# Head norms inside their own projections, and four joints between stages of a transformer pair on one Trainium2 core

## The chip, the cores and the metric

The kernel runs on 1 core of one Trainium2 chip. The metric is device time in microseconds from start to end of one execution on that core; the median over runs is given. Lower is better.

## The reference, cut to what matters

Two transformer blocks follow each other on 512 tokens of width 1024, all in fp32. The first block is a hybrid mixer (state space branch, dilated attention, pooling) with a feed-forward part; the second has four layers (window attention, latent attention, matrix LSTM, window attention) over 512 latent and 256 context tokens. The change touches four places of it:

```python
# first block, dilated attention: 12 heads of 128, each query and key head normed
qh = _rms(q.reshape(b, S, 12, 128), q_norm_w)
kh = _rms(k.reshape(b, S, 12, 128), k_norm_w)
# for each of 3 dilations: o, lse = attention(qh, kh, vh); then a softmax over the lse
# second block, every layer
h_l = rmsnorm(x_lat, g_pre) * (1.0 + sc_l) + sh_l
h_c = rmsnorm(x_ctx, g_pre) * (1.0 + sc_c) + sh_c      # over 256 context tokens
y_l, y_c = mixer(h_l, h_c)
x_lat = x_lat + gt_l * rmsnorm(y_l, g_post)
# layer 1, latent attention: two small norms ahead of two projections
q  = rmsnorm(q_a, g_qa) @ w_uq          # rank 256
kv = rmsnorm(kv_a, g_kva) @ w_ukv       # rank 128
o  = softmax(q k^T) v;   y = (o * silu(z)) @ w_out
# layer 3: y = (window_attention(rope(q), rope(k), v) * silu(z)) @ w_out, latent tokens only
```

## The kernel before, in words

All five engines run hand-written streams; they meet only through semaphores. Every fp32 product is made of three matmuls (`products`, L478 to L480): high part by high, high by low, low by high. ScalarE makes the high part of a weight slot of 2048 columns (`refill_hi`, L473), GpSimd the low part (L465), and SyncE's queue loads raw slots in a ring of three, each when TensorE is done with the slot before it in its place.

`dense` (from L508) is the projection routine. It walks over tiles; a tile is up to 512 columns by 8 chunks by 3 matmuls in one PSUM bank of a ring of `n_banks`. ScalarE copies each tile out (`act_tile`), which frees its bank (`tile_free`); refills of the coming slots stand at fixed tiles on ScalarE's queue. Guests (`Side`) put steps of their own behind tile t on each engine: `on_tensor`, `on_scalar`, `on_vector`, `within` (between the chunks of a tile), `early_scalar` (before the tile's copy), `after_vector`. `lead=2` computes the first two tiles together, chunk by chunk, and `rhs_ready` names a semaphore that a chunk of a tile has to wait for. `ada` puts the products of the modulation (L940 on VectorE, L871 for its transfers on ScalarE's queue) beside the tiles: ScalarE issues the next transfer, and copies the next tile, only when VectorE has used a place of the ring.

*First block, dilated attention* (`dilated_attention`, from L2000). Four projections j = 0 to 3 of 11 tiles each: tiles 0 to 5 are three query and three key heads, 6 to 9 values, 10 the rows of the third value head (`v_rows`), which TensorE has to transpose. Projections 0 and 1 host 8 and 4 slots of modulation. `HeadNorms` (from L1487) norms the six heads: squares on ScalarE (L1504), sums over partitions by a matmul with `ones` on TensorE (L1525), logarithm (L1510), exponential (L1515), the product on VectorE (L1543); it also transposes the V rows (L1530) and places them (L1538). The norms of projection j are the guest of projection j + 1, so those of 3 have no host: behind projection 3 the engines meet (`end_stage`, L383 to L402), walk through the eleven steps with filler matmuls around them (`keep_busy`, L381), and meet again. Then `group_attention` (from L1553) runs 16 units: scores (L1573), mask and minimum (L1617), exponential (L1639), scaling (L1630), transposes (L1581), copy (L1646), values (L1591).

*Into layer 0* (`LayerInBeside`, from L2708), guest of the last feed-forward projection: ScalarE squares the eight context chunks, VectorE adds them in SBUF (`tally_context`, L2753) behind tile 3, and TensorE sums the total over partitions in tile 4 behind chunk 2 (L2565). ScalarE then makes the root (L2571, L2572), and VectorE and ScalarE norm the context before VectorE takes tile 4 (L2367). VectorE also tallies the latent squares (L2745).

*Layer 1's joints.* `LatentSteps` (from L3276) makes the two small norms beside the projection of `z`: sums on TensorE (L3306) in banks 6 and 7, root 0 at its step 3, root 1 at step 5 (L1034, L1037; L3296 signals). `pair_attention` (from L1656) has 24 pairs of units; of the six pairs of two heads the fourth (last latent block) and the sixth (last context block) end with `finish` on VectorE (L3141, L753, L754: gate and split). Behind it TensorE runs 11 fillers (L1729) and all engines meet. Then `layer_cross` (from L3075) loads the residual (L3093), runs the projection `Bo` and crosses into the next layer.

*Layer 3's start of attention.* `AttentionStart` (from L1806) is the guest of the projection of `z` in 8 tiles: the scores of pairs 0 and 1 (L1879) behind tiles 4 and 5, VectorE's masks and minima (L1897) at tiles 5 and 6, four exponentials (L1913) behind the copy of tile 6, the first scaling (L1906) at tile 7. Window attention proper starts when tile 7 has been copied.

Of the kernel before, what the change touches and what calls it, by code (L numbers as in the profile page):

```python
# [23 lines left out]
P = 128  # L24
# [1462 lines left out]
class HeadNorms(Side):  # L1487
# [3 lines left out]
    STEPS = 11  # L1491

    def __init__(self, k, block, qkv, v, v_rows, squares, rstd, weights):
        self.k, self.qkv, self.v, self.v_rows = k, qkv, v, v_rows
        self.squares, self.rstd, self.weights = squares, rstd, weights
        self.squared, self.summed, self.logs, self.rooted, self.turned, self.normed = (
            k.sem_named(f"norm_{x}") for x in ("squared", "summed", "logs", "rooted", "turned", "normed"))

    def on_scalar(self, act, t):
        k = self.k  # L1500
        if t < 6:
            if t >= 2:
                act.wait_ge(self.summed.sem, self.summed.at(t - 1))
            act.activation(self.squares[:, t % 2], self.qkv[:, t, :], ACT.Square).then_inc(self.squared.sem, 1)  # L1504
        if t == 2 and self.normed.base:

            act.wait_ge(self.normed.sem, self.normed.at(0))
# [9 lines left out]
    def on_tensor(self, pe, t):  # L1517
        k = self.k
        if t == 1 and self.normed.base:
            pe.wait_ge(self.normed.sem, self.normed.at(0))  # L1520
        if 1 <= t < 7:
            pe.wait_ge(self.squared.sem, self.squared.at(t))
            if t >= 3:
# [3 lines left out]
        if t == 8:  # L1527
            pe.wait_ge(self.logs.sem, self.logs.at(5))
            for b in range(4):
                last = pe.transpose(k.psum[:, 6, b * P:(b + 1) * P], self.v_rows[:, b * P:(b + 1) * P],  # L1530
                                    k.cst("ident"))
            last.then_inc(self.turned.sem, 1)

    def on_vector(self, dve, t):
        k = self.k
        if t == 9:
            dve.wait_ge(self.turned.sem, self.turned.at(1))
            dve.tensor_copy(self.v[:, :, 256:384], k.psum[:, 6, :].rearrange("p (b n) -> p b n", b=4)) \  # L1538
                .then_inc(self.normed.sem, 1)
        if t == 10:  # L1540
# [5 lines left out]
    def over(self):  # L1546
        for x in (self.squared, self.summed, self.logs, self.rooted):
            x.stage_over(6)
        self.turned.stage_over(1)
        self.normed.stage_over(7)  # L1550


def group_attention(k, block, units, temp):  # L1553
# [6 lines left out]
    n, wide = len(units), 1280  # L1560
    row = k.at("group_row", temp, [P, 2, wide])
# [2621 lines left out]
```

## Time and profile before

| | |
|---|---|
| median of 3 runs | 2894.9 us (2893.01 to 2900.22) |
| the profiled execution's own time | 2897.45 us |
| its span, first to last instruction | 2895.7 us |
| granted TensorE clock, mean | 0.984 |
| TensorE busy | 2744.1 us, 95% |
| VectorE, ScalarE, GpSimd busy | 1555.8, 1231.5, 989.9 us |
| DMA | 293.73 MB, mean 101 GB/s |

Times in the views are microseconds from the first instruction. PE is TensorE, DVE VectorE, ACT ScalarE, POOL GpSimd. A name such as L1525 is the line of the kernel before. A TensorE row gives start and duration as modelled; matmuls overlap, so the distance of two starts tells what one costs. fp32 operands that are not split show as two records for each matmul. `[2.63 <-ACTq L3296]` at the end of a row: the engine stood idle for 2.63 us before it, until that was done.

### The profile page before, as it was taken

The numbers are of one execution on the slowest core, as the hardware profiler recorded it, in microseconds if no ns is written. First come the engines' busy times: TensorE is split into PE (matmuls) and PEld (weight loads), VectorE is DVE, ScalarE is ACT, GpSimd is POOL, SyncE is SP. The second block draws the span as 40 slices with busy tenths as digits, with TensorE's granted clock in tenths as the row PEclk, the third lists the DMA queues.
The fourth block names the chain that finished last, engine by engine and source line by source line (L and its number), as shares of the span: only waits on it lengthen the run. The fifth ranks groups of instructions, "written<-read, shape, count | busy, mean of one in ns | idle before, by whom it ended". The sixth has DMA issues, their size and how long they took to land.

```text
span 2895.7 us, 39337 instructions
## 1 busy us (share of the span) xinstructions
PE 2744.1 (95%) x15712; PEld 2268.5 (78%) x15712; DVE 1555.8 (54%) x3047; ACT 1231.5 (43%) x2139; POOL 989.9 (34%) x729
## 2 busy tenths in 40 slices
PE   6988989989999999999999999999999999999997
PEld 4766878868878888878977778677898878788785
DVE  6678292053653978772358451245446237752684
ACT  4335224554223322233268464544343236553682
POOL 3611565402545444433323333200234330143322
PEclk8999999999999999999999999999999999999998
DMA  8312462211232556633200121100221231124102
GB/s 320 134 42 85 174 258 88 88 44 44 102 131 102 218 204 233 218 117 113 98 30 2 59 88 73 58 1 1 92 98 59 95 124 48 70 88 138 45 2 73
DMA packets 54294, 293.73 MB, mean 101 GB/s; under 512 B 4512, under 2 KB 8928, under 8 KB 24288
## 3 DMA queue, kind: packets, MB, share of 16 engines
q1 hardware_dynamic: 22464, 163.59, 15.7%
q10 hardware_dynamic: 31648, 127.63, 11.7%
q8 instruction: 125, 2.05, 0.3%
q14 instruction: 57, 0.47, 0.0%
HBM read 268.10 MB, written 17.86 MB: 99 GB/s over the span
## 4 chain that ended last, share of the span: by engine, by line
PE 60%; DVE 6%; ACT 3%; issue 2%; POOL 1%; DMA 0%; PEldq 0%; PEld 0%; DVEq 0%; ACTq 0%; POOLq 0%
PE psum L478 15%; PE psum L480 15%; PE psum L479 15%; PE psum L1879 3%; PE psum L1926 2%; PE psum L1937 2%; PE psum L3924 2%; PE psum L1688 2%; PE psum L1711 2%; PE psum L1692 1%; PE psum L1700 1%; POOL w_lo L465 1%; DVE pair_row L1897 1%; DVE pair_prob L1906 1%; ACT pair_prob L1913 1%
## 5 line engine op out<-in xcount | busy, mean ns | idle before, releaser
L465 POOL TENSOR_TENSOR w_lo<-raw,w_hi 128x512 fp32r<-128x512 f32 x612 | 852.9, 1426 | 1569.0 <-ACT w_hi L473 1569.0
L478 PE MATMUL psum<-a_hi,w_hi 128*128 128x512 f32 (+2 forms) x1880 | 702.5, 374 | 32.6 <-DVE a_lo L1091 16.7
L479 PE MATMUL psum<-a_lo,w_hi 128*128 128x512 f32 (+2 forms) x1880 | 689.4, 367 | 0.0
L480 PE MATMUL psum<-a_hi,w_lo 128*128 128x512 f32 (+2 forms) x1880 | 689.3, 367 | 0.0
L478 PEld LDWEIGHTS psum<-a_hi,w_hi 128*128 128x128 f32 (+1 forms) x1880 | 355.2, 189 | 106.0 <-issue 17.9
L479 PEld LDWEIGHTS psum<-a_lo,w_hi 128*128 128x128 f32 (+1 forms) x1880 | 355.4, 189 | 61.6 <-issue 3.8
L480 PEld LDWEIGHTS psum<-a_hi,w_lo 128*128 128x128 f32 (+1 forms) x1880 | 355.0, 189 | 59.5
L473 ACT ACTIVATE w_hi<-raw 128x2048 fp32r<-128x2048 f32 x153 | 292.4, 1911 | 171.6 <-DMA raw<-stream 131.5
L478 PE MATMUL psum<-w_hi,a_hi 128*128 128x256 f32 (+1 forms) x608 | 196.6, 323 | 2.4 <-POOL w_lo L465 2.2
L940 DVE SCALAR_TENSOR_TENSOR ada_temp<-ada_ring,psum 128x1024 f32<-128x1024 f32 x160 | 185.7, 1217 | 18.0 <-ACT psum L1063 14.7
L479 PE MATMUL psum<-w_lo,a_hi 128*128 128x256 f32 (+1 forms) x608 | 192.4, 316 | 0.0
L480 PE MATMUL psum<-w_hi,a_lo 128*128 128x256 f32 (+1 forms) x608 | 192.4, 316 | 0.0
L1897 DVE CUSTOM_DVE_ANT_0 pair_row<-psum,pair_mask,neg_sinks 128x512 f32<-128x512 f32 (+1 forms) x160 | 115.8, 748 | 80.1 <-PE psum L1879 72.3
L940 DVE SCALAR_TENSOR_TENSOR ada_temp<-ada_ring,ada_rows 128x1024 f32<-128x1024 f32 x80 | 133.0, 1722 | 34.2 <-DVEq L1440 16.0
L1913 ACT ACTIVATE pair_prob<-pair_row,pair_stat 128x513 f32<-128x513 f32 (+1 forms) x160 | 114.7, 718 | 26.8 <-PE psum L1926 19.1
L478 PEld LDWEIGHTS psum<-w_hi,a_hi 128*128 128x128 f32 x608 | 115.8, 190 | 12.6 <-POOL w_lo L465 2.9
L479 PEld LDWEIGHTS psum<-w_lo,a_hi 128*128 128x128 f32 x608 | 115.8, 190 | 8.7 <-issue 1.4
L480 PEld LDWEIGHTS psum<-w_hi,a_lo 128*128 128x128 f32 x608 | 115.8, 190 | 7.6
L1879 PE MATMUL psum<-gk,gq 64*128 64x128 f32 (+1 forms) x960 | 95.3, 331 | 7.4 <-ACT gz L3174 3.9
L478 PE MATMUL psum<-hid_hi,w_hi 128*128 128x512 f32 x256 | 100.6, 393 | 0.0
L479 PE MATMUL psum<-hid_lo,w_hi 128*128 128x512 f32 x256 | 99.9, 390 | 0.0
L480 PE MATMUL psum<-hid_hi,w_lo 128*128 128x512 f32 x256 | 99.8, 390 | 0.0
(475 smaller groups left out, 4770.9 us busy)
## 6 DMA issues: line engine op xcount, KB each, us to landing
raw<-stream SPq DMA_DIRECT2D x153, 1024.0 KB, 4.8
ada_ring<-ada ACTq DMA_DIRECT2D x72, 1024.0 KB, 6.4
x_in<-xres ACTq DMA_DIRECT2D x3, 3072.0 KB, 10.3
xres<-x_in ACTq DMA_DIRECT2D x3, 2048.0 KB, 6.9
partner<-gq ACTq DMA_DIRECT2D x4, 1024.0 KB, 9.9
xres<-x_in ACTq DMA_DIRECT2D x1, 3072.0 KB, 9.3
own_raw<-stream SPq DMA_DIRECT2D x3, 1024.0 KB, 4.9
xres<-x_in ACTq DMA_DIRECT2D x3, 1024.0 KB, 4.9
```

Of the source, the lines that this page charges most:

```text
L465: last = pool.tensor_tensor(k.lo_of(s)[:, cols], k.raw_of(s)[:, cols], k.hi_of(s)[:, cols].bitcast(F32), ALU.subtract)
L473: act.activation(k.hi_of(s), k.raw_of(s), ACT.Copy).then_inc(k.hi_ready, 1)
L478: pe.matmul(out, lhs[0], rhs[0], start=start, stop=False)
L479: pe.matmul(out, lhs[0], rhs[1], start=False, stop=False)
L480: return pe.matmul(out, lhs[1], rhs[0], start=False, stop=stop)
L940: dve.scalar_tensor_tensor(self.temp[:, self.products % 2], self.ring[:, place, c], 1.0, self.used_rows[:, w], ALU.mult, ALU.mult, accum_o ...
L1688: pe.matmul(score(u)[:, col:col + cols], q, keys, start=True, stop=False)
L1711: last = pe.matmul(value_bank(u), units[u]["pv"][j], prob_t[:, u % n_t, j * P:(j + 1) * P], start=j == 0, stop=j == n_blocks - 1)
L1879: last = pe.matmul(score(u)[:, col:col + cols], q, keys, start=True, stop=True)
L1897: dve.tensor_tensor_reduce(row[:, u % 4, 1:1 + w], score(u), mask[:, un["mask"]:un["mask"] + w], 1.0, un["sink"], ALU.add, ALU.min, stat[: ...
L1913: act.activation(prob[:, u % 4, 0:1 + width(u)], row[:, u % 4, 0:1 + width(u)], ACT.Exp, bias=stat[:, 0, u % 4:u % 4 + 1], scale=-1.0, acc ...
L1926: last = pe.transpose(turn_place(u)[:, j * P:(j + 1) * P], prob[:, u % 4, 1 + j * P:1 + (j + 1) * P], k.cst("ident"))
```

## The change

It has six parts in the code.

1. `HeadNorms(j)` is now the guest of projection j itself. Its squares wait for the copy of their tile. The transposes of V rows leave it: they are made behind tile 0 of projection j + 1 (`turn_rows`, bank 7) and placed at tile 1 (`place_rows`); those of projection 3 inside `group_attention`, behind its first scores and ahead of the second unit on VectorE. The stage of its own, its two meetings and its 17 fillers are gone; the load of the attention's tables is issued between projections 2 and 3; the first scores wait for the norms of projection 3.
2. `tally_context` keeps its running sum in PSUM; the matmul over the total stands behind chunk 6 of tile 4, not 2.
3. `pair_attention` ends without fillers and meeting. The chunks of `Bo` wait for the `finish` that makes them, the residual's load for the last one, the weights' own slot for the last values; `Bo` computes its first two tiles together.
4. `LatentSteps` sums the second norm in banks 4 and 5 at step 3, and ScalarE makes both roots at step 4 (two logarithms each, one wait, the exponentials).
5. In layer 3 `AttentionStart` stands one tile later, and its first scaling comes behind the last tile.
6. `layer_cross` takes `lead` from its caller: 1 for layer 0 as before, 2 for `Bo`, 2 for `Co` as before.

The diff, cut to its core:

```diff
 class HeadNorms(Side):
@@ on_scalar
         if t < 6:
+            act.wait_ge(k.tile_free.sem, self.tile_free + t + 1)
             if t >= 2:
                 act.wait_ge(self.summed.sem, self.summed.at(t - 1))
             act.activation(self.squares[:, t % 2], self.qkv[:, t, :], ACT.Square).then_inc(self.squared.sem, 1)
@@ on_tensor
-        if t == 1 and self.normed.base:
-            pe.wait_ge(self.normed.sem, self.normed.at(0))
+        if t == 0 and self.rows_of is not None:
+            turn_rows(k, pe, self.rows_of, self.tile_free)
         if 1 <= t < 7:
             pe.wait_ge(self.squared.sem, self.squared.at(t))
+            if t == 2 and self.rows_of is not None:
+                pe.wait_ge(k.sem_named("rows_placed").sem, k.sem_named("rows_placed").at(1))
...
-        if t == 8:
-            pe.wait_ge(self.logs.sem, self.logs.at(5))
-            for b in range(4):
-                last = pe.transpose(k.psum[:, 6, b * P:(b + 1) * P], self.v_rows[:, b * P:(b + 1) * P],
-                                    k.cst("ident"))
-            last.then_inc(self.turned.sem, 1)
@@ on_vector
+        if t == 1 and self.rows_of is not None:
+            place_rows(k, dve, self.v_before)
         if t == 9:
-            dve.wait_ge(self.turned.sem, self.turned.at(1))
-            dve.tensor_copy(self.v[:, :, 256:384], k.psum[:, 6, :].rearrange("p (b n) -> p b n", b=4)) \
-                .then_inc(self.normed.sem, 1)
-        if t == 10:
             for r in range(6):
                 dve.wait_ge(self.rooted.sem, self.rooted.at(r + 1))
...
+def turn_rows(k, pe, rows, rows_in):
+    pe.wait_ge(k.tile_free.sem, rows_in)
+    for b in range(4):
+        last = pe.transpose(k.psum[:, 7, b * P:(b + 1) * P], rows[:, b * P:(b + 1) * P], k.cst("ident"))
+    last.then_inc(k.sem_named("rows_turned").sem, 1)
+
+def place_rows(k, dve, v):
+    turned = k.sem_named("rows_turned")
+    dve.wait_ge(turned.sem, turned.at(1))
+    dve.tensor_copy(v[:, :, 256:384], k.psum[:, 7, :].rearrange("p (b n) -> p b n", b=4)) \
+        .then_inc(k.sem_named("rows_placed").sem, 1)
@@ group_attention, scores(u)
             if u:
                 pe.wait_ge(masked.sem, masked.at(u))
+            else:
+                pe.wait_ge(*heads_normed)
+                pe.wait_ge(k.tile_free.sem, k.tile_free.at(-1))
...
         scores(0)
+        last_rows(pe)
...
+                if u == 1:
+                    last_placed(dve)
@@ pair_attention, end of TensorE's stream and of the stage
-        pe.wait_ge(masked.sem, masked.at(2 * n))
-        k.keep_busy(pe, k.psum[:, 0, :], 11)
...
-                pairs[p - 4]["finish"](dve)
+                pairs[p - 4]["finish"](dve).then_inc(finished.sem, 1)
...
-    k.end_stage(block)
+    return ends
@@ AttentionStart
+    def after_vector(self, dve):
+        if self.at + 3 >= self.n_tiles:
+            self.scale_probs(dve, 0)
@@ dilated_attention
-        dense(k, block, [f"qkv{j}"], tiles, act_tile=take, ada=ada.of((8, 4)[j]) if j < 2 else None, barrier=j == 3,
+        dense(k, block, [f"qkv{j}"], tiles, act_tile=take, ada=ada.of((8, 4)[j]) if j < 2 else None, barrier=False,
               n_banks=6, side=side)
...
-        k.keep_busy(pe, k.psum[:, 0, :], 6)
-        for t in range(side.STEPS):
-            side.on_tensor(pe, t)
-        k.keep_busy(pe, k.psum[:, 0, :], 11)
...
-    k.end_stage(block)
@@ LayerInBeside
-            so_far = self.squares_c[:, 0] if c == 1 else self.total_c[:]
-            dve.tensor_tensor(self.total_c[:], so_far, self.squares_c[:, c], ALU.add).then_inc(self.tallied_c.sem, 1)
+            so_far = self.squares_c[:, 0] if c == 1 else self.context.rstd
+            dve.tensor_tensor(self.total_c[:] if c == KC - 1 else self.context.rstd, self.squares_c[:, c], so_far,
+                              ALU.add).then_inc(self.tallied_c.sem, 1)
...
-        if (t, j) == (4, 2):
+        if (t, j) == (4, 6):
@@ gqa_layer, host
-              n_banks=n_banks, barrier=False, side=start(8 if both else 4, *steps))
+              n_banks=n_banks, barrier=False, side=start(8 if both else 5, 16 if both else 8, *steps))
@@ LatentSteps
-        if t in (3, 5):
-            r = t // 2 - 1
-            act.wait_ge(self.summed.sem, self.summed.at(r + 1))
-            root_rows(k, act, self.rstd[:, r], [LAT, CTX], (256, 128)[r], (6, 7))
-            act.nop().then_inc(self.rooted.sem, 1)
+        if t == 4:
+            act.wait_ge(self.summed.sem, self.summed.at(2))
...
-        if t in (1, 2, 4):
-            c = min(t - 1, 2)
+        if t in (1, 2, 3):
+            c = t - 1
             pe.wait_ge(self.squared.sem, self.squared.at(c + 1))
-            if c == 2:
-                pe.wait_ge(self.rooted.sem, self.rooted.at(1))
...
-        if t in (4, 6, 7):
-            c = {4: 0, 6: 1, 7: 2}[t]
+        if t in (5, 6, 7):
+            c = t - 5
@@ mla_layer
-    pair_attention(k, block, [pair_of(c, b) for c in range(4) for b in range(6)], R0 + 73728, 768)
-    return layer_cross(k, block, l, "Bo", b2, a, R0 + 49152, R0, R0 + 73728)
+    finished, values_done = pair_attention(k, block, [pair_of(c, b) for c in range(4) for b in range(6)], R0 + 73728,
+                                           768)
+    k.rhs_ready = {(j, KC * n): finished[j // 2 * 2 + n] for n in range(2) for j in range(KC)}
+    return layer_cross(k, block, l, "Bo", b2, a, R0 + 49152, R0, R0 + 73728, own_after=values_done,
+                       x_after=finished[-1], lead=2)
```

## Rows read from the trace of the kernel before

**Rows 1.** The page, part 4: the chain that ended last, by engine.

```profile
PE 60%; DVE 6%; ACT 3%; issue 2%; POOL 1%; DMA 0%; PEldq 0%; PEld 0%; DVEq 0%; ACTq 0%; POOLq 0%
```

**Rows 2.** Timeline, TensorE, end of projection 3 to the attention's first scores (start, duration).

```profile
586.25 0.39 PE L479 MATMUL psum<-a_lo,w_hi 128*128 128x512 f32 x1
586.47 0.39 PE L480 MATMUL psum<-a_hi,w_lo 128*128 128x512 f32 x1
...
601.06 4.91 PE L381 MATMUL psum<-const 128*128 128x256 f32 x22
607.88 0.94 PE L1573 MATMUL psum<-qkv 128*128 128x128 f32 x6 [1.90 <-DVEq L395]
```

**Rows 3.** Timeline, TensorE, a sum between 256-column matmuls in projection 3.

```profile
571.31 1.02 PE L1525 MATMUL psum<-squares,const 128*128 128x512 f32 x2
...
572.29 0.28 PE L479 MATMUL psum<-w_lo,a_hi 128*128 128x256 f32 x1
```

**Rows 4.** Timeline, ScalarE, projection 0: the copies of tiles 1 and 10.

```profile
373.65 0.60 ACT L2046 ACTIVATE qkv<-psum 128x512 f32<-128x512 f32 x1 [6.66 <-DVE ada_temp L940]
...
418.97 0.59 ACT L2048 ACTIVATE v_rows<-psum 128x512 f32<-128x512 f32 x1
```

**Rows 5.** TensorE's waits, 340 to 421 and 421 to 477 (total, times, longest).

```profile
PE psum L478 <- POOL w_lo L465: 5.5, 3, 3.1
...
PE psum L478 <- POOL w_lo L465: 4.9, 1, 4.9
```

**Rows 6.** Timeline, GpSimd, the low parts of two slots in projection 1.

```profile
421.45 17.17 POOL L465 TENSOR_TENSOR w_lo<-raw,w_hi 128x512 fp32r<-128x512 f32 x8 [9.99 <-ACT w_hi L473]
```

**Rows 7.** Timelines, ScalarE and VectorE: exponentials and products of projection 3's norms.

```profile
602.83 3.23 ACT L1515 ACTIVATE rstd<-rstd 128x512 f32<-128x512 f32 x6
...
603.49 2.08 DVE L1543 SCALAR_TENSOR_TENSOR qkv<-qkv,q_weight,rstd 128x512 f32<-128x512 f32 x3 [1.53 <-ACT rstd L1515]
```

**Rows 8.** The page, part 5: ScalarE's refills (busy, mean ns, idle before).

```profile
L473 ACT ACTIVATE w_hi<-raw 128x2048 fp32r<-128x2048 f32 x153 | 292.4, 1911 | 171.6 <-DMA raw<-stream 131.5
```

**Rows 9.** Adds by source line, before's form and the PSUM form (ns min/median/max).

```profile
L2753 DVE TENSOR_TENSOR total_c<-total_c,squares_c x6: 424/1296/1378, 1275.3 to 1281.5; 128x256 f32<-128x256 f32 x6
...
L3020 DVE TENSOR_TENSOR psum<-square_c,psum x18: 418/429/430, 1682.6 to 2593.7; 128x256 f32<-128x256 f32 x18
```

**Rows 10.** Timelines, TensorE and VectorE, around the context and latent sums.

```profile
1281.96 1.22 PE L2565 MATMUL psum<-total_c,const 128*128 128x256 f32 x2 [6.11 <-DVE total_c L2753]
...
1283.41 0.63 PE L479 MATMUL psum<-hid_lo,w_hi 128*128 128x512 f32 x1
...
1300.74 1.60 DVE L2745 TENSOR_TENSOR total<-total,squares 128x512 f32<-128x512 f32 x1 [0.70 <-ACT squares L2739]
...
1304.36 1.02 PE L2565 MATMUL psum<-total,const 128*128 128x512 f32 x2
```

**Rows 11.** Timelines, TensorE and VectorE, end of layer 1's attention.

```profile
2029.74 4.91 PE L381 MATMUL psum<-const 128*128 128x256 f32 x22
...
2030.47 0.69 DVE L754 TENSOR_TENSOR b_lo<-mq,b_hi 128x512 fp32r<-128x512 f32 x1
...
2035.11 0.47 PE L478 MATMUL psum<-b_hi,w_hi 128*128 128x512 f32 x1 [0.46 <-PEq L390]
```

**Rows 12.** Timeline, TensorE, the third sum of layer 1's small norms.

```profile
1776.50 2.05 PE L3306 MATMUL psum<-squares,const 128*128 128x512 f32 x2 [2.63 <-ACTq L3296]
```

**Rows 13.** Timelines, TensorE and ScalarE, start of layer 3's attention.

```profile
2712.91 2.50 PE L1879 MATMUL psum<-gk,gq 64*128 64x128 f32 x16 [3.42 <-ACT gz L3174]
...
2716.53 1.28 ACT L1913 ACT_TABLE_LOAD   x1 [3.68 <-PE psum L1926]
2717.83 0.83 ACT L1913 ACTIVATE pair_prob<-pair_row,pair_stat 128x641 f32<-128x641 f32 x1
```

**Rows 14.** Windows: PE, PEld, DVE, ACT, POOL busy (x), granted clock, DMA.

```profile
612.00:616.00 4.00, 3.23 (x9) 1.99 (x8) 2.53 (x11) 1.40 (x3) 0.00 (x0) 0.50 0.01 2
...
608.00:717.00 109.00, 101.22 (x574) 83.83 (x575) 52.96 (x192) 45.44 (x76) 15.50 (x12) 0.95 0.07 22
```

More of the change, by code:

```diff
@@ L1662, in pair_attention @@
                                            "out_done", "out_taken"))
+    finished = k.sem_named("pair_finished")
     n = len(pairs)
@@ L1797, in _ @@
                 take(p - 2)
+    n_finished = sum("finish" in pair for pair in pairs)
+    ends = [(finished.sem, finished.at(x + 1)) for x in range(n_finished)], (out_done.sem, out_done.at(2 * n))
+    finished.stage_over(n_finished)
     for s_ in (scores_done, out_taken):
@@ L3291, in on_scalar @@
             act.activation(self.squares[:, t], self.raw[:, t, :], ACT.Square).then_inc(self.squared.sem, 1)
-        if t in (3, 5):
-            r = t // 2 - 1
-            act.wait_ge(self.summed.sem, self.summed.at(r + 1))
-            root_rows(k, act, self.rstd[:, r], [LAT, CTX], (256, 128)[r], (6, 7))
-            act.nop().then_inc(self.rooted.sem, 1)
+        if t == 4:
+            act.wait_ge(self.summed.sem, self.summed.at(2))
+            rows = [(r, n, t0, t1) for r in range(2) for n, (t0, t1) in enumerate((LAT, CTX))]
+            for r, n, t0, t1 in rows:
+                k.act_chain.mark(act.activation(self.rstd[:, r, t0:t1], k.psum[:, 6 - 2 * r + n, 0:t1 - t0], ACT.Ln,
+                                                bias=k.eps[:], scale=1.0 / (256, 128)[r]))
+            act.wait_ge(k.act_chain.sem, k.act_chain.count)
+            for r, n, t0, t1 in rows:
+                last = act.activation(self.rstd[:, r, t0:t1], self.rstd[:, r, t0:t1], ACT.Exp, scale=-0.5)
+                if n:
+                    last.then_inc(self.rooted.sem, 1)
     def on_tensor(self, pe, t):
         k = self.k
-        if t in (1, 2, 4):
-            c = min(t - 1, 2)
+        if t in (1, 2, 3):
+            c = t - 1
             pe.wait_ge(self.squared.sem, self.squared.at(c + 1))
-            if c == 2:
-                pe.wait_ge(self.rooted.sem, self.rooted.at(1))
             for n, (t0, t1) in enumerate((LAT, CTX)):
-                last = pe.matmul(k.psum[:, 6 + n, 0:t1 - t0], k.cst("ones"), self.squares[:, c, t0:t1], start=c != 1,
+                last = pe.matmul(k.psum[:, (4 if c == 2 else 6) + n, 0:t1 - t0], k.cst("ones"), self.squares[:, c, t0:t1], start=c != 1,
                                  stop=c != 0)
@@ L3510, in finish @@
         def finish(dve):
-            for chunk in chunks:
-                chunk(dve)
+            chunks[0](dve)
+            return chunks[1](dve)
         return finish
```

73 lines of the change are left out of this document (38 added, 35 removed).

## The prediction

> **What bounds the kernel now.** The page's chain that ended last comes first: it lies on TensorE for 60% of the span, with 6% on VectorE and 2% "issue" [rows 1]. So the kernel is one long row of matmuls; another engine costs time only where TensorE stops for it, and a change is worth the gaps that it closes on TensorE, less the matmuls that it adds there. At each place that the diff touches I then read TensorE's timeline and waits, and after them the timeline of the engine that it waited for. In a full row the matmuls of 512 columns start 0.22 to 0.23 us apart (586.25, 586.47 [rows 2]); at 0.227 a dense tile of 24 takes 5.44 us, one of 256 columns 2.88.
>
> **Part 1: the head norms and their meeting.** Before, the norms of projection 3 have a stage of their own. The projection's last matmul starts at 586.47 (ends 586.70), the attention's first scores at 607.88: 21.2 us between [rows 2]. In it TensorE does six `ones` sums, four transposes and 17 fillers of which nothing is used (11 of them are the 22 records at 601.06 [rows 2]). A sum inside a row of 256-column matmuls costs 0.86 us: from its start (571.31) to the second matmul behind it (572.29) are 0.98, less one interval of 0.12 [rows 3].
> Removed: 21.2 us. Added: six sums, 5.2 us, since each projection now hosts its own norms: 1 to 3 exchange one set for another, 0 had none. What could hide them is the lateness of ScalarE in projection 0. It waits for VectorE's modulation products (tile 1 copied at 373.65 after 6.66 us of waiting for L940, tile 10 at 418.97 [rows 4]), so its weight copies come late, and TensorE waits 5.5 us around projection 0 and 4.9 us at the third tile of projection 1 for GpSimd's low parts [rows 5]. Arriving later it waits less. Followed in time: sum 1 wants the square behind tile 1 (373.65 + 0.60 + 0.62, at 375.0 with the signals) where TensorE stands at 372.9, a wait of 2.1; later squares and logarithms are there; tile 10 ends at 413, not 408; projection 1 starts then, stops for `turn_rows` until tile 10 is copied (about 420.5) and comes to its third tile at 427.3. The low part for it stood at about 430 (the first half of the 17.17 us from 421.45 [rows 6]). That is later now by what ScalarE has in front: six exponentials (3.23 us [rows 7]) and a table load (1.28 [rows 13]), most of which fits before VectorE lets tile 9 through; 0.9 us stays. So 0.9 in place of 5.2. VectorE gets six products (two groups of 2.1 us [rows 7]) ahead of its modulation products of projection 1; the last ring transfer, the copy of tile 1 and its square come 4 us later, and TensorE wants that square later still. SP's loads hang on finished tiles and move with them; the table transfer is issued before projection 3, in no one's way.
> At the end: exponentials and table load are done 4.5 us behind tile 8, the products 6.6 us; TensorE still has 2.9 + 5.4 us of tiles, so the wait on the norms costs nothing. The V rows' transposes wait for tile 10's copy, under `scores(0)` (0.94 us [rows 2]); they and VectorE's copy fit in the first units, where from 612 to 616 TensorE was busy 3.23 and VectorE 2.53 of 4.00 us [rows 14]. ScalarE has a refill (1.9 us [rows 8]) behind tile 10 ahead of the first exponential: between 0 and 1.9, I take 0.5, for the masking comes first. **21.2 - 0.9 - 0.5 = 19.8 us.**
>
> **Part 2: context sums through PSUM.** TensorE stops 6.11 us at L2565 for `total_c` [rows 10]. Six of the seven adds take a median 1296 ns; the form that the change uses takes 429 at L3020 [rows 9], so seven with their signals are 3.3 us, ready at 1277.7 in place of 1281.9. The sum moves behind 12 matmuls (2.7 us), to 1278.4: no wait. Behind the stop a matmul lasted 0.63 us (1283.41 [rows 10]) and not 0.39, the level of 1.2 GHz; 1.2 us in all. That makes 7.3. But VectorE's adds and tallies behind it come only 3.8 us earlier, since ScalarE's logarithm and tables bound the context's root: the last tally, over at 1302.3, moves to 1298.5, and the latent sum that wants it from 1304.36 [rows 10] to 1297.1. A new wait of 1.4 us and a relapse of the clock, 0.7. **5.2 us**, 3.8 to 7.3.
>
> **Part 3: the end of layer 1's attention.** The last value matmuls end at 2029.7; 11 fillers follow, then a meeting that waits for VectorE's finishing of both parts, and the projection starts at 2035.11 [rows 11]. Now it starts at 2029.7 and waits by chunk. The latent half of heads 6 and 7 is finished at 2031.16 [rows 11]; with two tiles together a chunk lasts 6 x 0.227 = 1.36 us, so chunk 6 is wanted at 2037.9; the context half eight tiles later. The residual's transfer on ScalarE's queue waits for that half: ScalarE stands there until 2033.5, and its first tile ends at 2040.6. **5.4 us.**
>
> **Part 4: layer 1's two roots.** The third sum waited 2.63 us for the first root [rows 12]; now it has banks of its own and goes a tile earlier. ScalarE does both roots in one pass, some 8 us, while TensorE has four tiles before it wants the next bank. Three table loads fewer, off the path. With the clock's relapse **2.9 us.**
>
> **Part 5: layer 3's attention starts a tile later.** ScalarE had four exponentials, a refill and a table load ahead of the last copy, for which TensorE waited 3.42 us, until 2712.91; then 2.50 us of scores, then transposes at 2715.4 [rows 13]. Now the copy comes at 2709.4 and the exponentials behind it; with a table load of 1.28 the first scaling stands at about 2713.6, the transposes follow, 1.7 us earlier, and the chain lacks the table load at 2716.53 [rows 13]. **2.2 us**, 1.7 to 2.8.
> The row says that a table switch holds ScalarE for 1.28 us. The Trainium skill (ScalarE: Activation LUTs, What ACT_TABLE_LOAD costs) counts about 1.38 us of drain on top, 2.66 a switch; by that figure, an estimate, this part would give 0.8 us and the sum 34.1. The trace has an exponential at 2717.83, right behind a load that ends at 2717.81 [rows 13], so the sum goes by the row.
>
> **The sum**: 19.8 + 5.2 + 5.4 + 2.9 + 2.2 = 35.5 us. The profiled execution took 2897.45 us, 1.75 around its span, and lies 2.6 above the median of 2894.9. Against its own time that is 2862.0, against the median 2859.4; I say 2860.
>
> **The rivals.**
> *The sums of projection 0 are not covered*: ScalarE's longer queue delays the refills as much as TensorE. Then 5.2 and 2.1 come on top, less the 0.9 counted: 2866. For it: 14 us more work for ScalarE there. Against: it idled 6.66 us before tile 1 alone. 0.15.
> *Gains given back at the next stop*: parts 2 and 5 run into chains of other engines, and projection 3's norms end late. Of 35.5, up to 5 of part 1 and all of 2 and 5 go: 2867 to 2872. 0.12.
> *The clock at the attention's start.* Granted clock 0.50 from 612 to 616, 0.95 over the whole attention [rows 14]: some ten us at the lower level, which cost about 4. Coming from full tiles, the dip may vanish or last as much longer: 2856 or 2864, inside my range.
> *Slower*: that dip, grown. Without fillers ahead of it, and with TensorE stopping for the masks in each unit, the lower level holds through the attention (608 to 717), whose 101.22 us of TensorE time [rows 14] nearly double. At two fifths of it, 38 us, the gain is gone; all of it gives about 2945. Against: with the same pattern of units the dip ended after ten us. 0.02. The Trainium skill (TensorE: Matmul & The Clock Gate, HAM oscillation) warns of this, bursts shorter than the waits between them, each starting slow; the rows bear it out for three units only.
> *The change doesn't do what it says*: some signal or bank lets `scores(0)` start late after all. Part 1 gives 12, the total 2867. 0.05.
>
> **How the numbers follow.** Forecast 0.66, its own range 2853 to 2867. The range goes up over the first two rivals and down by a vanished dip and a part 2 of 7.3: 2851 to 2873. A measurement of this kernel can tell about 0.3%, 8.7 us; every case but the slower one saves over 20: 0.96, 0.02, 0.02.
>
> **What would show it.** Under 1 us between projection 3's last L480 and the first L1573; TensorE's waits for `w_lo` in projections 0 and 1 near 5 us in all, not 10; `total_c` by adds of 0.43 us and a new wait of 1 to 2 us at the latent sum; `Bo`'s first L478 right behind the last L1711; no waits for the root at L3306 and for `gz`. Wrong would be: 3 us or more before the attention's first scores, a wait for `squares` or `rstd` at each tile of projection 0, a clock under 1.00 beyond the attention's first 12 us.

## The result, and the profile after

The changed kernel takes 2860.31 us (median of 4 runs, 2860.02 to 2862.8), the kernel before beside it 2894.28. The ratio on record is 0.9876, with a 95% interval of 0.9864 to 0.9888 (the two medians by themselves give 0.9883): 34 us less. Of the profiled executions the span fell from 2895.7 to 2858.2 us, by 37.5, where the prediction had a sum of 35.5. One execution of a kernel below, the profiled one of part 4 taken back, ran at a mean granted clock of 0.568 from end to end and took 4444.47 us; it is left out of all that follows, and that kernel was run again.

From the page of the changed kernel, the parts that answer to [rows 1]:

```profile
PE 2722.8 (95%) x15656; PEld 2251.8 (79%) x15656; DVE 1557.6 (54%) x3047; ACT 1225.9 (43%) x2134; POOL 991.6 (35%) x729
PE 60%; DVE 7%; ACT 3%; issue 2%; POOL 1%; DMA 0%; ACTq 0%; DVEq 0%; POOLq 0%
```

TensorE is as long a row as before, so a change of the whole is the sum of the gaps that closed on it. To see where, I compare the starts of the same instruction in both traces, from one landmark to the next; "earlier by" grows where the changed kernel gains.

| landmark | before | after | earlier by | gain of the stretch |
|---|---|---|---|---|
| projection 0, copy of tile 0 | 361.35 | 360.06 | 1.29 | 1.3, nothing changed there |
| projection 3, last L480 | 586.47 | 582.52 | 3.95 | **2.7** (part 1) |
| first scores of the attention | 607.88 | 582.75 | 25.13 | **21.2** (part 1) |
| weight copy behind the attention | 719.77 | 694.02 | 25.75 | **0.6** (part 1) |
| weight copy in the `out` projection | 835.18 | 811.47 | 23.71 | -2.0, nothing changed there |
| weight copy in layer 0 | 1310.18 | 1284.46 | 25.72 | **2.0** (part 2) |
| copy of `mz`, ahead of the roots | 1771.04 | 1745.68 | 25.36 | -0.4 |
| copy of `mz`, behind them | 1797.21 | 1767.35 | 29.86 | **4.5** (part 4) |
| layer 1's last values | 2028.55 | 1996.74 | 31.81 | 1.9, nothing changed there |
| weight copy in `Bo` | 2052.21 | 2014.99 | 37.22 | **5.4** (part 3) |
| weight copy in layer 2 | 2379.53 | 2343.97 | 35.56 | -1.7, nothing changed there |
| weight copy in layer 3 | 2841.28 | 2803.87 | 37.41 | **1.8** (part 5) |

Parts 1 to 5 gave 24.5, 2.0, 5.4, 4.5 and 1.8 us where 19.8, 5.2, 5.4, 2.9 and 2.2 were forecast. The unchanged places add up to -0.9.

**The meeting**, TensorE's timeline of the changed kernel, in place of [rows 2]:

```profile
582.52 0.39 PE L480 MATMUL psum<-a_hi,w_lo 128*128 128x512 f32 x1
582.75 0.83 PE L1591 MATMUL psum<-qkv 128*128 128x128 f32 x6
583.60 0.66 PE L1555 MATMUL psum<-const,v_rows 128*128 128x128 f32 x4
584.70 1.56 PE L1591 MATMUL psum<-qkv 128*128 128x256 f32 x6 [0.45 <-DVE group_stat L1644]
586.96 0.55 PE L1599 MATMUL psum<-const,group_row 128*128 128x128 f32 x3 [0.70 <-DVE group_row L1653]
588.78 2.42 PE L1591 MATMUL psum<-qkv 128*128 128x256 f32 x6 [1.27 <-DVE group_stat L1644]
```

The scores follow the projection's last product by 0.23 us, one interval; the transposes of V rows stand right behind them.

**Projections 0 and 1.** First TensorE's waits of the changed kernel from 340 to 480 us (us in total, times, longest), then windows of it (window, length, busy time and count by engine, granted clock, DMA share, GB/s):

```profile
PE psum L1530 <- ACT squares L1506: 2.5, 1, 2.5
PE psum L478 <- POOL w_lo L465: 2.3, 1, 2.3
PE psum L1555 <- ACT v_rows L2078: 1.2, 1, 1.2
```
```profile
410.00:415.00 5.00, 5.00 (x24) 4.14 (x23) 5.00 (x7) 1.44 (x2) 0.90 (x1) 1.00 0.67 233
430.00:435.00 5.00, 5.00 (x23) 3.80 (x21) 5.00 (x6) 1.83 (x4) 5.00 (x3) 1.00 0.38 116
```

The same two windows of the kernel before, and two more of it for parts 2 and 4 below:

```profile
410.00:415.00 5.00, 3.48 (x9) 2.83 (x10) 5.00 (x9) 0.38 (x1) 1.46 (x1) 0.66 0.61 229
430.00:435.00 5.00, 5.00 (x12) 3.92 (x13) 5.00 (x5) 0.00 (x0) 5.00 (x3) 0.50 0.15 62
1275.00:1285.00 10.00, 3.89 (x11) 2.83 (x10) 7.47 (x8) 2.91 (x4) 5.47 (x4) 0.66 0.24 98
1775.00:1780.00 5.00, 3.50 (x7) 2.18 (x8) 3.54 (x4) 4.80 (x6) 1.57 (x1) 0.66 0.51 198
```

Before, `w_lo` cost 10.4 us here [rows 5]; now 2.3. The third tile of projection 1 comes out of its stop at 428.60, before at 429.80, or 428.51 with the 1.29 of the start taken off: six sums more, and 0.1 us later. And behind the stop before, a granted clock of 0.50 for the whole of 430 to 435 (the level of 1.2 GHz), where the changed kernel has 1.00. I count what a lower clock costs as the length of the window times what is missing to 1.00, here 5.00 x 0.50 = 2.5 us.

**The context's sum and what comes behind it.** Timeline of the changed kernel: VectorE's adds and TensorE's sum, ScalarE's square and weight copy, GpSimd's low part, TensorE's first product of layer 0:

```profile
1252.65 1.50 DVE L2777 TENSOR_TENSOR psum<-squares_c,psum 128x256 f32<-128x256 f32 x3 [0.48 <-DVE psum L2777]
1254.25 0.42 DVE L2777 TENSOR_TENSOR total_c<-squares_c,psum 128x256 f32<-128x256 f32 x1
1254.73 0.70 PE L2589 MATMUL psum<-total_c,const 128*128 128x256 f32 x2
1266.11 0.47 ACT L2610 ACTIVATE a_hi<-psum,mod 128x256 fp32r<-128x256 f32 x1 [0.44 <-DVE psum L2605]
1267.80 0.63 ACT L2763 ACTIVATE squares<-x_in 128x512 f32<-128x512 f32 x1 [1.21 <-DVE x_in L2391]
1268.34 1.90 ACT L473 ACTIVATE w_hi<-raw 128x2048 fp32r<-128x2048 f32 x1
1270.31 10.84 POOL L465 TENSOR_TENSOR w_lo<-raw,w_hi 128x512 fp32r<-128x512 f32 x8 [13.35 <-ACT w_hi L473]
1276.24 0.39 PE L478 MATMUL psum<-a_hi,w_hi 128*128 128x256 f32 x1 [3.77 <-POOL w_lo L465]
```

The seven adds run in PSUM and take 4.0 us from the first start to the last end (1250.68 to 1254.67), where 3.3 were forecast and 7.5 were spent before; the sum comes without a wait, so the stop of [rows 10] is gone. But 18 us later TensorE stands 3.77 us for the weights of layer 0's first projection: their high part is copied behind the context's norms on ScalarE. The clock stands at 0.83 from 1275 to 1285, 1.7 us.

**The other joints**, the same timeline: part 3 (no filler, no meeting), part 4 (a copy, then both logarithms, both exponentials), part 5:

```profile
1996.74 1.35 PE L1737 MATMUL psum<-pair_prob_t,mv 128*128 128x128 f32 x8
1997.85 0.47 PE L478 MATMUL psum<-b_hi,w_hi 128*128 128x512 f32 x1
1751.54 1.99 ACT L3321 ACTIVATE rstd<-psum,eps 128x512 f32<-128x512 f32 x4
1754.85 1.77 ACT L3325 ACTIVATE rstd<-rstd 128x512 f32<-128x512 f32 x4
2674.55 1.28 ACT L1944 ACT_TABLE_LOAD   x1
2675.85 0.72 ACT L1944 ACTIVATE pair_prob<-pair_row,pair_stat 128x513 f32<-128x513 f32 x1
2674.59 1.37 PE L1910 MATMUL psum<-gk,gq 64*128 64x128 f32 x16 [0.69 <-ACT gz L3199]
2678.15 1.09 PE L1957 MATMUL psum<-const,pair_prob 128*128 128x128 f32 x8 [2.19 <-DVE pair_prob L1937]
2680.15 2.08 PE L1910 MATMUL psum<-gk,gq 64*128 64x128 f32 x12 [0.91 <-DVE pair_stat L1928]
```

Between 1749 and 1774 no wait is left on TensorE, and its clock is 1.00. At part 5 the wait for `gz` fell from 3.42 us to 0.69; it is not gone, as the prediction's list of signs had it.

### The profile page after: what moved, and what is told of

It reads as the page before. It is cut to its first block, busy times and chain, and to the rows that moved or that the text cites. A ratio compares the mean times of both kernels' runs of the same rounds, so it can differ in the third digit from the quotient of the medians.

```text
span 2858.2 us, 39219 instructions
## 1 busy us (share of the span) xinstructions
PE 2722.8 (95%) x15656; PEld 2251.8 (79%) x15656; DVE 1557.6 (54%) x3047; ACT 1225.9 (43%) x2134; POOL 991.6 (35%) x729
## 4 chain that ended last, share of the span: by engine, by line
PE 60%; DVE 7%; ACT 3%; issue 2%; POOL 1%; DMA 0%; ACTq 0%; DVEq 0%; POOLq 0%
PE psum L478 15%; PE psum L480 15%; PE psum L479 15%; PE psum L1910 3%; PE psum L1957 2%; PE psum L1968 2%; PE psum L3956 2%; PE psum L1714 2%; PE psum L1737 2%; PE psum L1718 1%; PE psum L1726 1%; POOL w_lo L465 1%; DVE pair_row L1928 1%; DVE pair_prob L1937 1%; DVE c_decay L4074 1%
## 5 line engine op out<-in xcount | busy, mean ns | idle before, releaser
L480 PE MATMUL psum<-a_hi,w_lo 128*128 128x512 f32 (+2 forms) x1880 | 687.9, 366 | 0.0
L480 PEld LDWEIGHTS psum<-a_hi,w_lo 128*128 128x128 f32 (+1 forms) x1880 | 354.6, 189 | 59.2
L480 PE MATMUL psum<-w_hi,a_lo 128*128 128x256 f32 (+1 forms) x608 | 193.1, 318 | 0.0
L480 PEld LDWEIGHTS psum<-w_hi,a_lo 128*128 128x128 f32 x608 | 116.1, 191 | 7.7
L480 PE MATMUL psum<-hid_hi,w_lo 128*128 128x512 f32 x256 | 99.6, 389 | 0.0
## 6 DMA issues: line engine op xcount, KB each, us to landing
x_in<-xres ACTq DMA_DIRECT2D x3, 3072.0 KB, 10.4
```

What stands on the lines that cost most here:

```text
L480: return pe.matmul(out, lhs[1], rhs[0], start=False, stop=stop)
```

## The experiments

Each was run beside the kernel before, whose median beside them was 2898.0, 2898.7 or 2896.2 us. For small effects the traces are the better measure: between two kernels that differ in one place, all landmarks ahead of it agree but for the clock's dips, so the shift just ahead of the place is taken off the shift just behind it.

### Part 1 taken back

```diff
-        v, side = values(j), norms(j)
+        v = values(j)
...
-        dense(k, block, [f"qkv{j}"], tiles, act_tile=take, ada=ada.of((8, 4)[j]) if j < 2 else None, barrier=False,
+        dense(k, block, [f"qkv{j}"], tiles, act_tile=take, ada=ada.of((8, 4)[j]) if j < 2 else None, barrier=j == 3,
               n_banks=6, side=side)
+        if side is not None:
+            side.over()
+        side = norms(j)
```

With it come back the stage of its own and its fillers, as in the change's diff with the signs turned.

> The changed kernel with part 1 taken back (the norms of projection 3 in a stage of their own, two meetings, 17 fillers), parts 2 to 5 kept. Theory A, read from the two traces: part 1 is worth 24 to 25 us (21.2 between the last matmul of projection 3 and the first scores, 2.6 in projections 0 and 1, the rest in the attention), so this kernel takes about 2885 us, and its trace has waits for w_lo of about 10 us around projections 0 and 1 again and a stretch at a granted clock of 0.5 to 0.6 at the attention's start. Theory B, the prediction's step: part 1 is worth 19.8, so 2880; the rest of the difference then came from places that the change does not touch and would stay here.

2884.58 us, ratio 0.9958 (0.9943 to 0.9973). Its trace is 0.88 us later than the changed kernel's at the copy of tile 0 of projection 0, where the two do not differ yet. With that taken off it is 2.1 us later at the end of projection 3, 25.5 at the weight copy behind the attention and 23.4 at the last weight copy. Waits for `w_lo` from 340 to 480: 11.7 us. The attention starts at 606.92 here and at 582.75 in the changed kernel; the 20 us with the start in them, this kernel first:

```profile
600.00:620.00 20.00, 14.88 (x52) 10.11 (x50) 12.05 (x40) 7.18 (x13) 0.00 (x0) 0.74 0.00 0
```
```profile
580.00:600.00 20.00, 15.83 (x84) 11.41 (x82) 14.50 (x51) 9.14 (x14) 5.24 (x4) 1.00 0.22 85
```

Theory A holds: part 1 is worth about 24, not 19.8. Of the 25.5, 1.4 are given back in the `out` projection, where TensorE waits for `x_lo` in either kernel.

### Fillers in projection 0 of the kernel before

```diff
+    def on_tensor(self, pe, t):
+        if 1 <= t < 7:
+            self.k.keep_busy(pe, self.k.psum[:, 6, :], 2)
```

The class with these lines is the guest of projection 0, which had none.

> The kernel before with 12 filler matmul pairs (0.45 us each, 5.4 us in all) behind tiles 1 to 6 of projection 0, where the change puts its six sums; nothing of their result is used. Theory A: TensorE is early there and waits for the low parts of weights (10.3 us around projections 0 and 1), so the fillers are covered: the time stays within 1 us of the kernel before, the waits for w_lo shrink to about 5 us, and fewer stretches at a lower granted clock may even give 1 to 2 us. Theory B (the prediction's first rival): what TensorE does more delays what it waits for: 5 us slower. The prediction's step says 0.9 slower.

2898.28 us beside 2897.99, ratio 0.9998 (0.9989 to 1.0008). In the traces the weight copy at 317.62 comes 2.95 us earlier in this execution than in the one of before, and so do the copy at 419.45 and the last of projection 3: 5.4 us of matmuls cost nothing. TensorE's waits from 340 to 480 in this kernel:

```profile
PE psum L478 <- POOL w_lo L465: 6.9, 2, 6.2
```

A first half of the mistake in part 1: the covered work is free to the last 0.1 us. The waits shrink by 3.5 us only, to 6.9 where about 5 were expected: the clock of 0.66 that before has from 410 to 415 is 1.00 here, and the 1.7 us that this saves turn into waiting. The medians differ by less than their scatter.

### Projection 0's sums made twice

```diff
+            if self.rows_of is None:
+                pe.matmul(k.psum[:, 6 + (t - 1) % 2, :], k.cst("ones"), self.squares[:, (t - 1) % 2], start=True,
+                          stop=True)
```

> The changed kernel with each of projection 0's six sums made twice, 5.2 us more of TensorE's work. Theory A (the low parts of weights set the pace there): of the 5.2 us the stops at the rows' transposes (1.2) and at projection 1's third tile (2.3) take up 3.5, so 1.7 us slower, about 2862. Theory B (what TensorE does more delays the others as much): 5.2 slower, 2865.5.

2858.63 us, ratio 0.987 (0.9855 to 0.9885), beside 2861.26 for the changed kernel: no cost. Against the changed kernel's first trace it is 0.97 us early at 316.51 and 0.86 at 437.53, so 5.2 us cost 0.1. Its waits from 340 to 480:

```profile
PE psum L1531 <- ACT squares L1506: 1.6, 1, 1.6
PE psum L478 <- DVE acc L1443: 0.9, 1, 0.9
```

Theory A said 1.7 and was still too high: the stop at the first square shrinks too (2.5 to 1.6), which I had left out, and with the 3.5 that makes 4.4. Where the other 0.7 are covered was not looked into. The rival that the sums are not covered is out, by two kernels.

### Part 2 taken back

```diff
-            so_far = self.squares_c[:, 0] if c == 1 else self.context.rstd
+            so_far = self.squares_c[:, 0] if c == 1 else self.total_c[:]
-        if (t, j) == (4, 6):
+        if (t, j) == (4, 2):
```

> The changed kernel with part 2 taken back (sum of the context squares in SBUF, its matmul behind chunk 2). Theory A, from the traces: the stop of 6.1 us for total_c comes back and the stop of 3.8 us for w_lo at the head of layer 0's first projection goes, each with its stretch at a lower clock, so this kernel is 2.0 us slower than the changed one, 2862.3. Theory B, the prediction's step: 5.2 us slower, 2865.5.

2863.07 us, ratio 0.9883 (0.9866 to 0.9899). Just ahead of the place its trace agrees with the changed kernel's to 0.1 us; behind it (1284.46 against 1287.14) it is 2.7 later. `w_lo` is not waited for there; `total_c` is, 5.7 us. So part 2 is worth 2.0 by one pair of traces and 2.7 by the other, not 5.2: theory A. The pairs differ by the clock: over the ten us behind the stop for `total_c` it is 0.85 in before and 0.73 here.

### The weight copy ahead of the context's norms

```diff
             self.context.root(act)
+            refill_hi(self.k, act, self.early_slot)
             for c in range(KC):
                 self.context.take_high(act, c)
```

The same copy is taken out of the list of refills, where it stood behind tile 4.

> The changed kernel with one weight copy on ScalarE (the first slot of layer 0's first projection) moved from behind tile 4 to between the context's root and its first high part, 9 us earlier in time. Theory A: the stop of 3.8 us for w_lo goes, but the copy's 1.9 us delay the context's norms and, behind them on VectorE, the latent tallies, so TensorE stops for the tallies at the latent sum instead, for about 3.4 us: gain 0 to 0.5 us, about 2860. Theory B: the low part alone set that stop; then 3.8 us and the 1.7 us of lower clock behind it go: 2855.

2855.35 us, ratio 0.9856 (0.9842 to 0.9871). Its timeline:

```profile
1259.58 1.91 ACT L473 ACTIVATE w_hi<-raw 128x2048 fp32r<-128x2048 f32 x1
1274.68 1.13 PE L2592 MATMUL psum<-total,const 128*128 128x512 f32 x2 [1.29 <-DVE total L2772]
```

What stopped TensorE was indeed that copy. Neither theory had the size. The latent tallies are the next limit, as A says, but at 1.29 us and not 3.4: VectorE, though its context part ends 1.4 us later, ends the tallies 0.4 us earlier. Most of that is the length of the adds themselves. In the changed kernel GpSimd makes `w_lo` from 1270.31 on, and VectorE's last two adds of 512 columns, at 1270.79 and 1273.51, last 1.37 and 1.55 us; here GpSimd has done that slot from 1261.56 to 1266.61 and rests until 1275.78, and the same adds last 0.69 each. One of the two in the changed kernel, and the two here:

```profile
1273.51 1.55 DVE L2769 TENSOR_TENSOR total<-total,squares 128x512 f32<-128x512 f32 x1 [0.69 <-ACT squares L2763]
```
```profile
1271.89 0.69 DVE L2772 TENSOR_TENSOR total<-total,squares 128x512 f32<-128x512 f32 x1 [0.70 <-ACT squares L2766]
1273.94 0.69 DVE L2772 TENSOR_TENSOR total<-total,squares 128x512 f32<-128x512 f32 x1 [0.69 <-ACT squares L2766]
```

The rest is a square that comes 0.3 us sooner. The gain at the place is 4.1 us: 0.24 later than the changed kernel ahead of it, 3.85 earlier behind (1284.46 against 1280.61).

### ... and the tallies a tile later

```diff
-        if t >= 2:
+        if t in (2, 3):
             self.tally(dve, t - 1)
+        elif t > 4:
+            self.tally(dve, t - 2)
...
     def after_vector(self, dve):
+        self.tally(dve, KC - 2)
```

> The kernel of context_refill_early, and from tile 4 on VectorE tallies a latent square one tile later, behind the take of the next tile, so that it does not wait 0.7 us for ScalarE's square each time. Theory A: the stop of 1.3 us at the latent sum, all that is left there, is set by VectorE's chain; it shrinks by 0.9 to 1.3 us and what follows comes 1 us earlier, about 2854.5. Theory B: ScalarE's last square, which the second latent sum wants, becomes the end of the chain: no gain, 2855.4.

2852.86 us, ratio 0.985 (0.9836 to 0.9865), the fastest, though its times (2850.75 to 2855.75) overlap those of the kernel before it (2853.1 to 2859.78). The stop at the latent sum is 0.94 us in place of 1.29, and the place gains 0.4, less than A said: the last tally now stands behind the take of tile 7, and that take waits 0.46 us for TensorE itself, so nothing is left there that VectorE's order alone could give. Against the changed kernel beside it (2861.26) it is 8.4 us less; the traces put 4.5 of that at this place. Two dips of the clock are missing elsewhere, at 1835 to 1855 and around 2320, worth about 1.6 us each; nothing in the edit explains them.

### Part 3 taken back, and its meeting without fillers

```diff
+        pe.wait_ge(masked.sem, masked.at(2 * n))
+        k.keep_busy(pe, k.psum[:, 0, :], 11)
...
+    k.end_stage(block)
```

With them go the waits of `Bo` by chunk and its first two tiles together. The second kernel lacks the line with `keep_busy`.

> The changed kernel with part 3 taken back (11 fillers and a meeting behind layer 1's attention, Bo one tile at a time). Theory A, the prediction's step, which the traces bear out from the last value matmuls to Bo's second tile: 5.4 us slower, 2865.7. Theory B: the whole shift between layer 1's small norms and Bo (7.0 us) belongs to part 3: 2867.3; by theory A the other 1.6 lie ahead of the attention's end and don't come back here.

> The kernel of joint_undone without the 11 filler matmul pairs ahead of the meeting: TensorE stands idle for those 5.4 us. Theory A: the stop costs the same 5.4 us, and the first few us of Bo run at the lower clock for it, as behind the stops of 6.1 and 4.9 us in the trace of before: 1 to 2.5 us slower than joint_undone, about 2867.5. Theory B: the clock doesn't care about one stop: the same time as joint_undone.

With fillers 2866.38 us, ratio 0.9893 (0.9877 to 0.991). From the last values to the weight copy in `Bo` it loses 5.4 us on the changed kernel (2.53 later at 1999.27, 7.96 at 2022.95). Theory A. Bare 2869.05, ratio 0.9902 (0.9885 to 0.9918); its timeline and windows:

```profile
2006.57 0.76 PE L478 MATMUL psum<-b_hi,w_hi 128*128 128x512 f32 x1 [3.91 <-DVEq L395]
```
```profile
2006.00:2009.00 3.00, 2.43 (x6) 1.97 (x7) 0.65 (x2) 0.00 (x0) 0.00 (x0) 0.50 0.56 169
2009.00:2014.00 5.00, 5.00 (x18) 3.92 (x17) 0.00 (x0) 0.00 (x0) 0.00 (x0) 0.71 1.01 407
```

The meeting itself is over sooner without fillers (`Bo` starts 5.26 us behind the last values' start, with them 6.57), but `Bo` then runs at 0.50 and 0.71, where the kernel with fillers has 1.00, and at its weight copy the kernel is 1.2 us behind. So theory A of the clock, at the low end of its size. The medians alone (2.7 us apart, ranges overlapping) would not show it.

### Parts 4 and 5 taken back

```diff
-        if t == 4:
+        if t in (3, 5):
+            r = t // 2 - 1
...
-        side=start(8 if both else 5, 16 if both else 8, *steps)
+        side=start(8 if both else 4, *steps)
```

The first lines are of part 4's kernel (one root a step, all sums in banks 6 and 7), the last two of part 5's.

> The changed kernel with part 4 taken back (layer 1's second small norm in the banks of the first, its root one pass later). Theory A, from the traces: the stop of 2.6 us for the first root comes back, and behind it 1.7 us of lower clock: 4.5 us slower than the changed kernel, 2864.8. Theory B, the prediction's step: 2.9 slower, 2863.2.

> The kernel of roots_undone once more, for a trace at the full clock. Theory A: the stop of 2.6 us at the third sum and 1.7 us of lower clock behind it, 4.5 us slower than the changed kernel. Theory B, the prediction's step: 2.9 us slower.

> The changed kernel with part 5 taken back (layer 3's first scores behind tiles 4 and 5, the exponentials ahead of the last copy). Theory A, the prediction's step and the traces: 1.8 to 2.2 us slower, about 2862.2, TensorE waiting 3.4 us for gz again. Theory B, with 2.66 us a table switch: 0.8 slower, 2861.1.

The first kernel was run twice: 2865.89 and 2863.72 us (0.9893, 0.9876 to 0.991; 0.9888, 0.9872 to 0.9905). In the second trace the stop is back, and the clock behind it:

```profile
1750.07 2.65 PE L3331 MATMUL psum<-squares,const 128*128 128x512 f32 x4 [2.63 <-ACTq L3321]
```
```profile
1750.00:1755.00 5.00, 4.93 (x13) 3.28 (x14) 4.90 (x5) 3.58 (x3) 3.01 (x2) 0.66 0.31 133
```

From 1.1 us early at 1735.97 it goes to 3.5 late at 1778.75: 4.6 us, theory A. The medians would not decide it: the second is 2.5 us above the 2861.26 of the changed kernel beside it, the first 5.6 above the 2860.31 of the first result. In this trace two dips that the changed kernel's first trace has in layer 2, at 2315 to 2325 and 2465 to 2475 (0.83 each), are missing, which hides 3.4 of the 4.6. The other, 2863.56 us (0.9884, 0.9869 to 0.9899), is 0.5 us later than the changed kernel's trace ahead of layer 3's attention (2655.14) and 2.3 behind it (2803.87): 1.8 us, theory A.

### The changed kernel once more

> The changed kernel itself once more, to have its time beside the others' and a second trace of it: 2860 to 2863 us. The stretches at a lower granted clock behind unchanged stops are expected elsewhere than in its first trace, each shifting what follows by 1 to 2 us; the stops themselves the same to 0.1 us.

2861.26 us (2857.99 to 2864.97), ratio 0.9879 (0.9864 to 0.9894). Windows of this execution, then of the first one of the same kernel:

```profile
421.00:431.00 10.00, 7.70 (x29) 5.59 (x28) 9.59 (x8) 2.25 (x2) 10.00 (x6) 0.92 0.40 147
431.00:441.00 10.00, 10.00 (x40) 7.82 (x39) 10.00 (x14) 6.24 (x7) 6.30 (x4) 0.91 0.29 107
580.00:600.00 20.00, 15.99 (x71) 10.98 (x69) 14.07 (x48) 7.61 (x14) 5.25 (x4) 0.91 0.27 102
```
```profile
421.00:431.00 10.00, 7.69 (x33) 5.68 (x32) 9.59 (x10) 2.96 (x4) 9.88 (x6) 1.00 0.41 148
431.00:441.00 10.00, 10.00 (x44) 7.75 (x42) 10.00 (x12) 6.53 (x8) 7.94 (x5) 1.00 0.31 107
580.00:600.00 20.00, 15.83 (x84) 11.41 (x82) 14.50 (x51) 9.14 (x14) 5.24 (x4) 1.00 0.22 85
```

The same stop of 2.31 us for `w_lo`, to the hundredth, and once the clock falls behind it, once not; the same in the attention's first units. Each dip shifts what follows by 1.3 to 1.6 us. One stop differs, against what was expected: the 1.2 us for the V rows is not there. The clock is 0.83 from 370 to 380 in this execution, so TensorE comes later and finds the rows ready.

## Why the prediction was right, and where not

The total (2860, measured 2860.3) and the range were right, but that the total came out to the microsecond is luck: two errors of some size cancelled in it, 4.7 us in part 1 and 3.2 in part 2.

**Part 1, meeting: right.** 21.2 us between the last product and the first scores were forecast and measured. The wait on the norms costs nothing, the transposes of V rows lie where they were put, and the masking comes ahead of the late exponential.

**Part 1, projections 0 and 1: the step "so 0.9 in place of 5.2" failed**, by 3.6 us: the stretch gained 2.7. The third tile was forecast 0.9 later than before and came 0.1 later (428.60 against 428.51 with the start taken off). The 0.9 that ScalarE's exponentials were to add did not appear: two traces have the stop end at the same time, and neither 5.4 us of fillers nor doubled sums moved it. The larger share is the clock: behind the stop of 4.9 us TensorE ran five us at 0.50, 2.5 us of time, and I costed the stop without what stands behind it, which in part 2 I had counted. The 2.7 is also the better of two cases: in three of the traces with part 1 the clock falls behind the stop of 2.31 us too, and there the stretch gains 1.6 less. I forecast waits near 5 us for `w_lo`; 2.3 were left, the rest of the time lying in the stops at the square (2.5, forecast 2.1) and at the rows (1.2).

**Attention's start: -0.5 forecast, 0.6 in fact.** The rival of the clock's dip was open between 2856 and 2864; it fell to the good side, but for less than its 4 us. Over the attention's first 20 us the clock is 0.74 in all three traces without part 1; with it, it is 1.00 in eight of ten and 0.91 in two. From the first scores to the weight copy the attention takes 111.9 us before and 111.3 after, since a later dip (0.79 from 652 to 660) stands in the changed kernel; in the one trace without any dip, that of part 5 taken back, it takes 109.7. That later dip is also one of the prediction's signs of being wrong, a clock under 1.00 beyond the attention's first 12 us: it came, within eight us, and cost about 1.5. The slower rival, the lower level all through the attention, did not come; its two figures do not fit each other either (38 us for two fifths make 95 for all of it, about 2955 and not 2945). The rule on bursts shorter than their waits (the Trainium skill, TensorE: Matmul & The Clock Gate, HAM oscillation) is not put to the test here: TensorE is busy 15.83 of the 20 us from 580 to 600, and what the traces show are single dips.

**Part 2: the step "the latent sum ... a new wait of 1.4 us and a relapse of the clock, 0.7" failed.** I followed the tallies and not the weights. The new stop stands ahead of that sum, 3.77 us for `w_lo`, with 1.7 us of lower clock: 2.0 to 2.7 us are left of the 5.2. The moved copy shows the cause (the stop is gone, 4.1 us gained), and that my tally was the limit right behind it (1.29 us). The rival "gains given back at the next stop" held here, for part 2 alone.

**Part 3: right,** 5.4 forecast, 5.4 in both pairs of traces.

**Part 4: mis-sized**, 2.9 against 4.5 and 4.6: the stop of 2.6 is as forecast, but the relapse behind it is 1.7 us (granted clock 0.66 over five us), for which I had put 0.3.

**Part 5: nearly right**, 2.2 against 1.8 in both pairs. The transposes start at 2678.15, which is 1.6 us earlier than before once the 35.6 of the shift are taken off; the load drops out of the chain. Missing in the forecast were a wait of 0.91 us for VectorE at the next scores and the clock, over ten us from the scores on 0.72 before and 0.83 in the changed kernel. That a table switch holds ScalarE 1.28 us is seen again: load at 2674.55, exponential at 2675.85. By the 2.66 of the Trainium skill (ScalarE: Activation LUTs, What ACT_TABLE_LOAD costs) the part would have given 0.8, by the prediction's estimate; the trace with it taken back says 1.8.

**The sum:** 4.7 too little for part 1, 3.2 too much for part 2, 1.6 too little for part 4, 0.4 too much for part 5, together 2.7 too little; unchanged places took 0.9 back. That leaves about the 2 us by which the span beat the 35.5.

## What to carry to other kernels

A stop of TensorE costs its length and the lower clock behind it, here 1.5 to 3.1 us over the ten us behind the stops of 2.6 to 6.2 us at the changed places (clock 0.85 to 0.69); behind the stop of 2.31 us it was nothing in six of nine traces and 1.6 in three. Price both, and fill such a stop or close it whole. Before a wait is taken away, list every input of the work right behind it, the weights' own copies too: the next stop may be one whose producer stands behind the moved work in its queue, and moving that one copy (4.1 us) was worth more than what was left of the part that it had cut down (2.0 to 2.7). Work put on an engine that arrives early costs nothing up to its slack, which the waits of the stage show.

## What the runs showed of the hardware

The granted clock behind one and the same stop is not the same in each execution. The changed kernel twice had a stop of 2.31 us at projection 1; behind it the clock stayed at 1.00 in one execution and stood at 0.92 and 0.91 for two stretches of ten us in the other. The like explains the unchanged places of the first table: in layer 1's attention the kernel before has two stretches of 20 us at 0.91 and the changed one has one (1.9 us gained), and in layer 2 the changed kernel alone has 0.83 from 2315 to 2325 (1.7 lost). The loss of 2.0 in the `out` projection is less clear: the stop for `x_lo` and a dip are in both kernels (clock 0.83 over ten us before, 0.68 after). The projection takes 115.4 to 116.0 us in the three traces without part 1 and 117.2 to 117.6 in nine of the ten with it, but 115.4 in the tenth, that of part 5 taken back. So it is not more work: the second wait for `x_lo` is 0.83 us in the changed kernel, 0.26 before and 0.22 in that tenth trace, and the dip behind it is deeper. Why this mostly comes with part 1 stays open.

Eleven fillers in a bare meeting hold up the next projection by 1.3 us and save 2.5 us of lower clock: worth 1.2 us net by one pair of traces, where no way is found to drop the meeting, which is worth 5.4.

VectorE's adds with both inputs in SBUF lasted longer while GpSimd was making `w_lo`: 1.37 and 1.55 us in place of 0.69 for 512 columns at one and the same place, with and without GpSimd at work beside it. The six adds of [rows 9] show the same. GpSimd is at work from 1275.63 to 1281.10; the four adds that start in that time last 1.30 to 1.38 us each, the one ahead of it (1275.27) lasts 0.42 and the one behind it (1281.48) 0.43. The changed kernel's adds of the same size with an operand in PSUM last 0.42 or 0.43 with GpSimd at work beside them (1251.92 to 1256.97). So what part 2 gained on VectorE is that its adds no longer slow down beside GpSimd.
